# RWKV value projection in three rounded passes on one Trainium2 core

## The reference, cut to what matters

```python
    def mix(c):
        return h + dx_p * mu_prev[c] + dx_n * mu_next[c]
    xw, xa, xg = mix(1), mix(4), mix(5)
    r = mix(0) @ w_r
    k = mix(2) @ w_k
    v = mix(3) @ w_v
    kk = heads(k * k_k)
    kk = kk / jnp.maximum(jnp.sqrt(jnp.sum(kk * kk, axis=-1, keepdims=True)), 1e-12)
```

## Time and profile before

| what | value |
|---|---|
| median of 3 runs | 2331.82 us (2328.57 to 2337.57) |
| the profiled execution, its own time | 2330.63 us |
| its span | 2328.8 us |
| granted TensorE clock, mean | 0.986 |
| TensorE busy | 2209.9 us (95%), 20900 matmuls |
| VectorE busy | 1230.6 us (53%) |
| ScalarE busy | 935.8 us (40%) |
| GpSimd busy | 711.2 us (31%) |

### The profile page before, as it was taken

The page is one execution under the profiler, slowest core; times in us unless marked ns, Lnnn a source line. Parts: engine busy times, 40 slices in busy tenths (PEclk is TensorE's granted clock), DMA queues, the critical chain, the costliest instruction groups (busy, mean ns, idle before and its releaser), DMA issues.

```text
span 2328.8 us, 48362 instructions
## 1 busy us (share of the span) xinstructions
PE 2209.9 (95%) x20900; PEld 1688.0 (72%) x20900; DVE 1230.6 (53%) x1833; ACT 935.8 (40%) x1553; POOL 711.2 (31%) x380
## 2 busy tenths in 40 slices
PE   7999989999989998889889889999999999999998
PEld 6885778888877647778777777788887666753486
DVE  5118344013248676667666433794225999727123
ACT  4238444233325434455544453564332122352133
POOL 2310233444420103222222134444442333420245
PEclk9999999999989999999999999999999999999999
DMA  4312122233222210000000122343222333222232
GB/s 146 115 60 82 55 73 91 90 100 99 91 70 90 83 41 12 11 10 11 11 11 4 39 83 89 117 181 126 90 91 97 111 109 118 91 81 75 70 100 82
DMA packets 49889, 180.77 MB, mean 78 GB/s; under 512 B 5600, under 2 KB 5856, under 8 KB 49440
## 3 DMA queue, kind: packets, MB, share of 16 engines
q1 hardware_dynamic: 46064, 166.82, 21.7%
q10 hardware_dynamic: 3632, 11.08, 1.2%
HBM read 167.33 MB, written 10.55 MB: 76 GB/s over the span
## 4 chain that ended last, share of the span: by engine, by line
PE 77%; issue 10%; DVE 7%; POOL 3%; ACT 2%; DMA 0%; POOLq 0%; DVEq 0%; ACTq 0%
PE ps L651 16%; PE ps L652 16%; PE ps L653 16%; PE ps L654 6%; PE ps L934 2%; POOL ring_lo L2539 2%; PE ps L997 2%; PE ps L882 1%; PE ps L704 1%; PE ps L1220 1%; PE ps L988 1%; PE ps L1140 1%; PE ps L796 1%; PE ps L811 1%; PE ps L786 1%
## 5 line engine op out<-in xcount | busy, mean ns | idle before, releaser
L2539 POOL TENSOR_TENSOR ring_lo<-ring,ring_hi 128x1024 fp32r<-128x1024 f32 x228 | 555.8, 2445 | 1001.4 <-ACT ring_hi L1277 1001.4
L653 PE MATMUL ps<-u_lo,ring_hi 128*128 128x512 f32 x968 | 384.2, 397 | 0.0
L1277 ACT ACTIVATE ring_hi<-ring 128x1024 fp32r<-128x1024 f32 x240 | 251.2, 1052 | 96.7 <-DMA ring<-in_wall 93.1
L654 PE MATMUL ps<-arena,ring 128*128 128x512 f32 x480 | 210.5, 594 | 6.0 <-ACT arena L1775 3.3
L653 PEld LDWEIGHTS ps<-u_lo,ring_hi 128*128 128x128 f32 x968 | 183.5, 190 | 43.3
L651 PE MATMUL ps<-mlp_u_hi,ring_hi 128*128 128x512 f32 x512 | 204.4, 399 | 10.2 <-DVE u_lo L1944 8.7
L651 PE MATMUL ps<-mid_hi,ring_hi 128*128 128x512 f32 x512 | 204.0, 399 | 2.6 <-POOL ring_lo L2539 2.6
L653 PE MATMUL ps<-mid_lo,ring_hi 128*128 128x512 f32 x512 | 203.9, 398 | 0.0
L652 PE MATMUL ps<-mid_hi,ring_lo 128*128 128x512 f32 x512 | 203.7, 398 | 0.0
L652 PE MATMUL ps<-mlp_u_hi,ring_lo 128*128 128x512 f32 x512 | 203.5, 397 | 0.0
L651 PE MATMUL ps<-in_u_hi,ring_hi 128*128 128x512 f32 x480 | 193.3, 403 | 6.7 <-DVE u_lo L2409 3.7
(11 more groups left out here) (461 smaller groups left out, 4270.2 us busy)
## 6 DMA issues: line engine op xcount, KB each, us to landing
ring<-in_wall SPq DMA_DIRECT2D x273, 512.0 KB, 3.7
s_tables<-arena ACTq DMA_DIRECT2D x16, 512.0 KB, 3.0
arena<-s_tables SPq DMA_DIRECT2D x16, 512.0 KB, 3.8
arena<-bias_lines SPq DMA_DIRECT2D x16, 448.0 KB, 4.3
arena<-in_lora SPq DMA_DIRECT2D x8, 384.0 KB, 3.1
h<-in_x SPq DMA_DIRECT2D x1, 2048.0 KB, 8.4
out<-arena ACTq DMA_DIRECT2D x8, 256.0 KB, 2.8
consts<-in_consts SPq DMA_DIRECT2D x1, 1152.0 KB, 14.4
```

The source lines that it names most:

```text
L653: return nc.tensor.matmul(y, w_hi, low, start=False, stop=x == k - 1)
L654: return nc.tensor.matmul(y, ring[:, at:at + P], rhs(x), start=x == 0, stop=x == k - 1)
L1277: nc.scalar.activation(ring_hi[:, slot], ring[:, slot], ACT.Copy).then_inc(sem("weights_high"), 1)
L2539: G.tensor_tensor(ring_lo[:, slot], ring[:, slot], ring_hi[:, slot].bitcast(F32), ALU.subtract).then_inc(sem("weights_split"), 1)
```

## The change

`rv` joins the projections made in three rounded passes. Its eight weight blocks are split: the high parts by ScalarE, the low part of the first by VectorE and of the other seven by GpSimd. Its mixed input (m = 5) is split by ScalarE and VectorE into two buffers that r's and k's mix parts used before. ScalarE's new work stands in its order as the diff shows: split_high of blocks 0, 1 and 2 and eight mix_highs ahead of kk_square 0, split_high of block x + 3 ahead of the take of tile x. TensorE waits for an input tile's two parts where it waited for the mixed tile.

```diff
-SPLIT = {"qk", "v", "attn_out", "r", "k", "o", "w_in", ...
+SPLIT = {"qk", "v", "attn_out", "r", "k", "rv", "o", "w_in", ...
+LOW_BY_VECTOR += [FIRST_BLOCK["rv"]]
-        mix_parts = {0: (r_mix_hi, r_mix_lo), 2: (k_mix_hi, k_mix_lo)}
+        v_mix_hi, v_mix_lo = r_mix_lo, k_mix_lo
+        mix_parts = {0: (r_mix_hi, r_mix_lo), 2: (k_mix_hi, k_mix_lo), 5: (v_mix_hi, v_mix_lo)}
@@ TensorE
-                    if name == "rv":
-                        beside_values(j, x)
+                def value_parts(j, x):
+                    if j == 0:
+                        parts_ready(x)
+                    beside_values(j, x)
+                elif name == "rv":
+                    high, low = mix_parts[m]
+                    dense(name, lambda x: (tile(high, x), tile(low, x)), rhs_ready=value_parts)
@@ ScalarE
             def take_value(x):
+                if x + 3 < DT:
+                    split_high(FIRST_BLOCK["rv"] + x + 3)
                 take_tile("rv", x, tile(vTr, x))
             mix_starts(5)
+            split_high(FIRST_BLOCK["rv"])
             take_tile("lora_a", 0, lo_a)
+            split_high(FIRST_BLOCK["rv"] + 1)
+            for x in range(DT):
+                mix_high(5, x)
+            split_high(FIRST_BLOCK["rv"] + 2)
             act.wait_ge(y_taken, FIRST_TILE["lora_g"])
             kk_square(0)
             kk_square(1)
@@ VectorE
-                for x in range(DT + 1 + 2 * (m == 2)):
+                for x in range(DT + 1 + 2 * (m in (2, 5))):
-                    if m == 2 and x >= 3:
+                    if m in (2, 5) and x >= 3:
                         mix_low(m, x - 3)
+                    if m == 5 and x == 4:
+                        split_low("rv", 0)
@@ GpSimd
-            for name in ("r", "k"):
+            for name in ("r", "k", "rv"):
                 for x in range(DT):
                     if FIRST_BLOCK[name] + x not in LOW_BY_VECTOR:
                         split_low(FIRST_BLOCK[name] + x)
```

More of the change, by code:

```diff
@@ L66 @@
 ]
-SPLIT = {"qk", "v", "attn_out", "r", "k", "o", "w_in", "up0a", "down0a", "up0b", "down0b", "up1a", "down1a", "up1b", "down1b",
+SPLIT = {"qk", "v", "attn_out", "r", "k", "rv", "o", "w_in", "up0a", "down0a", "up0b", "down0b", "up1a", "down1a", "up1b", "down1b",
          "w_out", "ple", "gate"}
```

## The result

The changed kernel takes 2336.51 us (median of 20 runs, 2330.45 to 2347.12), the one before 2331.57 us beside it (20 runs, 2326.55 to 2337.57). The ratio is 1.0022, with a 95% interval of 1.0014 to 1.0031: 5.1 us slower (3.3 to 7.2), where +1.5 was forecast. The profiled execution of the changed kernel was the lowest of its runs, 2330.45 us, and its span, 2328.7 us, can't be told from that before. So the spans don't show where the 5 us lie. k ends 2.4 us earlier in that execution (786.66 against 789.10), in identical work, at other granted clocks on the way (0.79 against 0.74 from 660 to 700), and from there to the end of the span it is 1542.0 us after and 1539.7 before.

What follows compares the result with a forecast made beforehand. Bound: TensorE through rv, then GpSimd's features up to 870.82, waiting for Exps behind rv's tile 6. Pause +8.6, clock +1.9, saving -9.0 gave +1.5: 2332.1 us profiled, 2333.3 on the median; range 2325 to 2341.

Steps and rivals of the forecast that it cites:

- Saving per product: rv on TensorE: three passes take 0.70 us instead of 0.86, saving 6.7 us to head norm 7, 9.0 to tile 6.
- The pause ahead of rv: Work queued on ScalarE ahead of lora_g's take makes TensorE start rv at 818.5 instead of 809.96, 8.6 us later.
- The port meeting: Ahead of rv, GpSimd's split of block 1 holds up VectorE's mix_low 0 over SBUF: done at 804.0, not 802.1.
- Rival A: Ahead of rv: ScalarE and VectorE get through in time, TensorE never waits; 2322.8 us, chance 0.11.
- The clock behind the pause: At rv's start the granted clock falls after TensorE's idle time; loss 1.7 to 3.0 us, taken as 1.9.
- rival C: At rv's start: the pause is as forecast but the clock stays; -0.4 net, 2331.4 us, chance 0.07.
- Inside rv [...] nothing waits: In rv's tiles of 6.75 us, ScalarE's and GpSimd's splits of later blocks finish before use, so nothing waits.
- it has 5.06 and keeps up: VectorE's kk chain inside rv needs 4.44 us a tile, has 5.06 and keeps up with 0.6 to spare.
- The later arm decides: +1.5: GpSimd's L2572 comes at 871.8 through kk's chain or 872.3 through rv's tile 6; the later decides, +1.5 us.
- rv's own end [...] stays covered: The end of rv on TensorE moves by 8.6 + 1.9 - 10.2 = +0.3 us and stays covered.
- GpSimd's row runs on by itself: Behind L2572, GpSimd's row of feature products runs on by itself, so +1.5 us is the whole delay.
- Rival B: Inside rv: GpSimd's splits hold up VectorE's reciprocals, so the kk chain becomes the bound; +8.8, 2340.6 us, chance 0.10.

Runs made afterwards that it cites:

- The experiments on ScalarE's order: Changed kernel, ScalarE's queue ahead of rv: block 2's split later, 1.0023; three mix_highs earlier, 2333.08 us; both, 0.9995; whole row in another order, 0.9958.
- the reordered kernel: Changed kernel with ScalarE's row ahead of rv in another order, lora_a's take first, nothing added or left out: 2324.98 us, ratio 0.9958 to the kernel before.
- the one-operand experiment: Changed kernel, VectorE's kk product reading one operand from PSUM in place of SBUF (kk becomes zero): ratio 1.0011 to the kernel before.
- the kernel with the moved splits: The reordered kernel with split_high of blocks 4 to 7 queued ahead of kk_root 2, 3, 4 and 6: ratio 0.9971 to the kernel before.
- the first experiment: Changed kernel with nine dead fp32 products on TensorE filling the pause between lora_g and rv: ratio 1.0002 to the kernel before.
- the fill in the reordered kernel: The reordered kernel plus five dead products on TensorE between the first pair's two directions' scores: ratio 0.9959 to the kernel before.
- the second experiment: Changed kernel with nine dead products ahead of rv and four more between the first pair's two directions: ratio 1.0010 to the kernel before.

## Why the prediction was right, and where it was off

The kernel got slower, as forecast, and for the reasons given ahead of rv; but the size was 5.1 us where 1.5 was said, and two steps behind that point failed. The +1.5 was what is left of +10.5 and -9.0, so the sign was a close call. It isn't luck alone, though: on the arm through tile 6, where the missed terms don't enter, the traces have +2.1. Step by step:

- **Saving per product:** right. Records 0.233 us apart, norms 5.06 apart, 6.7 us up to norm 7.
- **The pause ahead of rv:** right in size (+8.8 against +8.6) and in cause. The experiments on ScalarE's order take 1.0, 0.6, 4.0 and 8.4 us off it by moving only what is queued there. The port meeting was on another instruction than said, at the same price. Two small slips in the working cost nothing: 797.6 less 797.0 is 0.6 and not 0.8 us of TensorE's wait (measured 0.51), and 796.1 and 3.5 make 799.6 and not 799.9. Rival A fails with it; the reordered kernel, which puts kk_square and the takes ahead of block 2's split as A demanded, comes near that case.
- **The clock behind the pause:** right, 2.2 us where 1.9 was taken from bounds of 1.7 to 3.0. The filled pause gives them back; rival C fails.
- **"Inside rv [...] nothing waits", and of VectorE, "it has 5.06 and keeps up":** this step failed. VectorE has 0.6 us to spare a tile, and a meeting with a split costs 1.4. From 829.59 to GpSimd's start it is the chain's only engine. From head norm 7 to GpSimd's first product it took 14.9 us (67.2 to 82.1), where 14.1 less 1.1 was forecast: 1.9 us more. The step looked for the meeting only in the reciprocal, which is the long instruction, and not in the product behind it, which reads two operands of SBUF like the rows of the meeting that the prediction itself had quoted.
- **"The later arm decides: +1.5":** tile 6's take came at 80.5 us after k, where before had 78.4: +2.1 (said +1.5). It wasn't the arm that decided. kk's arm was, at +3.2 for the third product. In the one-operand experiment, where kk's arm is shortened, the third product waits for the Exps again, 1.7 us earlier than after (0.6 of it by the clock).
- **"rv's own end [...] stays covered", and "GpSimd's row runs on by itself":** true of rv's end, +0.8 where +0.3 was said. What was missed is that GpSimd's row moves while rv's end doesn't. So this step failed too. TensorE's wait for the second direction grew from 1.52 to 4.27 us, the clock fell a second time, and with 0.4 us by which GpSimd's row was late, the second pair came 2.1 us later still. The step took the third product's delay for the delay of all behind it.

Rival B named the right place, the kk chain beside GpSimd's splits, and the wrong instruction. Its +8.8 charged each reciprocal with a whole split; measured were four products at 1.4, 1.4, 1.4 and 0.8 us, partly inside VectorE's spare time. The Trainium skill (SBUF — State Buffer, Who interferes with whom) says that an instruction of VectorE with at most one SBUF input, outside its two-port modes, doesn't contend with GpSimd, while one with two does against a GpSimd instruction that reads SBUF. The traces agree on both: reciprocals of 3.34 us beside splits, products of 2.05 with two SBUF operands and 0.63 with one. The prediction had used the rule to clear the reciprocal and not gone on to the next instruction of the chain.

The sum as measured: +8.8 and +2.2 less 6.7 make +4.3 at norm 7. The way from there to GpSimd's first product is 0.7 us longer than before (14.9 against 14.2), which makes +5.0. The wait for the Exps behind it (1.8 us) is gone, which makes +3.2 at the third product. 0.4 of GpSimd's row and 1.7 of the second fall make +5.3 at the second pair, which is the size of the timed 5.1.

Three things are open. The first is what becomes of the 5.3 us behind the second pair, since the two traces reach the o projection 0.3 us apart the other way round. The second is why the reordered kernels with and without the fill are timed 4 to 5 us better than their traces' distances say (the kernel with the moved splits gains 6.8 by its times and 6.9 by its trace), and the first experiment 2.6 better. The third is what the second fall costs by the times rather than in the trace.

## What to carry to other kernels

When an operation is made cheaper by work on other engines, first write down what is now queued ahead of the operation's own start on each of those engines: here a saving of 10.2 us became a loss of 5.1 with an order in which the first product's bank was released last, and the same work in another order gained 6.5 to 13.1 us. For every new GpSimd instruction that reads SBUF, go through all of VectorE's instructions beside it by their number of SBUF operands, the short ones too: here the reciprocal of 3.34 us went free and the product of 0.65 paid 1.4. And when a covering block of TensorE's work gets shorter than the chain beside it gets later, look for the wait that opens behind it, and for the clock in that wait. Last, a distance in one trace that has the size of the timed difference isn't yet its explanation: follow it to the end of the stage.

## What the runs showed of the hardware

The granted clock can be at 1.2 GHz although TensorE is fully busy: with the fill in the reordered kernel it was 0.50 from 869 to 872 at 3.00 us of work in 3.00, having fallen 0.3 us after the fill began, while with the fill of the second experiment it stayed at 1.00. So a filler isn't a sure cure, and where it fails it runs at half rate itself. The loss to the clock behind rv's pause was 2.2 us after an idle time of 7.95 us, and still 1.6 us after one of 3.99. The clock also falls without a long pause: in the execution before it fell at 969.7, and the longest wait of TensorE in the 12 us ahead was 1.81 us, while behind a wait of 1.52 us at 880 it stayed at 1.00.

VectorE's 128x512 product with two SBUF operands takes 0.65 us alone and 2.05 beside a GpSimd split, and its reciprocal with one takes 3.34 us in both cases. The splits beside them take 2.38 or 2.39 us.
